# Gathering the running sums into the product's buffer instead of accumulating in the transfer, with 2 MB expert-weight loads

## The reference, cut to what matters

```python
N_EXPERTS, TOP_K, D_FF = 32, 4, 1024      # of 1024 features
# each token's 4 best experts, with softmax gates; for expert e and its tokens:
#   gu  = rows @ w_gate_up[e] + b_gate_up[e]          (1024 -> 2048)
#   a   = clamped swiglu of the even and odd columns  (-> 1024)
#   moe[token] += gate * (a @ w_down[e] + b_down[e])  (1024 -> 1024)
h = layernorm(ALPHA * h + moe)
```

## Time and profile before

| | |
|---|---|
| median of 3 runs | 2167.34 us (2166.53 to 2167.43) |
| profiled execution | 2166.51 us |
| its span, first to last instruction | 2164.7 us |
| TensorE busy | 2074.1 us (96%) |
| VectorE, ScalarE, GpSimd busy | 1304.2, 942.7, 478.6 us |
| mean granted TensorE clock | 0.988 |
| moved by DMA | 540.45 MB, mean 250 GB/s |

### The profile page before, as it was taken

The page is one execution under the profiler, slowest core; times in us unless marked ns, Lnnn a source line. Parts: engine busy times, 40 slices in busy tenths (PEclk is TensorE's granted clock), DMA queues, the critical chain, the costliest instruction groups (busy, mean ns, idle before and its releaser), DMA issues.

```text
span 2164.7 us, 28230 instructions
## 1 busy us (share of the span) xinstructions
PE 2074.1 (96%) x10156; PEld 1542.5 (71%) x10156; DVE 1304.2 (60%) x1467; ACT 942.7 (44%) x1117; POOL 478.6 (22%) x453
## 2 busy tenths in 40 slices
PE   8999999989999998999999999989999999999998
PEld 5778876655566655566655788777777879888887
DVE  7567687664446654456554899873786456423435
ACT  5236354544334553335453677643445423322420
POOL 4261158651212111213322222100220010000000
PEclk9999999999999999999999999999999999999999
DMA  5140177999999999999999999942312333232321
GB/s 202 45 154 21 62 260 309 397 401 414 399 408 408 403 408 408 408 403 411 405 416 407 399 393 382 341 164 79 100 45 79 117 110 124 78 117 78 117 78 39
DMA packets 107513, 540.45 MB, mean 250 GB/s; under 512 B 13012, under 2 KB 14164, under 8 KB 56608
## 3 DMA queue, kind: packets, MB, share of 16 engines
q1 hardware_dynamic: 95184, 507.96, 58.8%
q0 software_dynamic: 9760, 26.47, 4.9%
q10 hardware_dynamic: 2480, 4.80, 0.7%
HBM read 519.26 MB, written 22.28 MB: 250 GB/s over the span
## 4 chain that ended last, share of the span: by engine, by line
PE 75%; DMA 13%; DVE 7%; ACT 2%; issue 1%; POOL 0%; ACTq 0%; DVEq 0%; SPq 0%; POOLq 0%
PE PS L465 71%; DMA ring<-w_down 13%; DVE low L2531 2%; ACT act_parts L1887 1%; PE PS L805 1%; PE PS L880 1%; PE PS L674 0%; DVE st L2283 0%; DVE act_parts L2627 0%; DVE act L2646 0%; DVE act L2642 0%; PE PS L1269 0%; DVE small L2465 0%; PE PS L809 0%; PE PS L473 0%
## 5 line engine op out<-in xcount | busy, mean ns | idle before, releaser
L465 PE MATMUL PS<-act_parts 128*128 128x512 f32 (+2 forms) x2208 | 680.7, 406 | 54.6 <-DVE low L2531 44.1
L2531 DVE TENSOR_TENSOR low<-ring,act_parts 128x2048 fp32r<-128x2048 f32 x224 | 504.8, 2298 | 206.6 <-ACT act_parts L1887 205.9
L1887 ACT ACTIVATE act_parts<-ring 128x2048 fp32r<-128x2048 f32 x228 | 430.3, 1916 | 241.2 <-DMA ring<-w_down 176.8
L465 PEld LDWEIGHTS PS<-act_parts 128*128 128x128 f32 (+2 forms) x2208 | 395.8, 192 | 154.7 <-DVE low L2531 47.4
L465 PE MATMUL PS<-act_parts,ring_parts 128*128 128x512 f32 (+3 forms) x1696 | 466.8, 374 | 0.0
L465 PE MATMUL PS<-low,act_parts 128*128 128x512 f32 x960 | 382.7, 399 | 0.0
L465 PEld LDWEIGHTS PS<-act_parts,ring_parts 128*128 128x128 f32 (+1 forms) x1696 | 302.2, 187 | 67.0 <-issue 13.3
L465 PE MATMUL PS<-ring,act 128*64 128x512 f32 (+1 forms) x1274 | 288.9, 595 | 0.0
L465 PE MATMUL PS<-ring_parts,act_parts 128*128 128x512 f32 (+2 forms) x1208 | 271.0, 381 | 2.1 <-DVE act_parts L3030 2.1
L465 PEld LDWEIGHTS PS<-ring_parts,act_parts 128*128 128x128 f32 (+1 forms) x1208 | 218.3, 187 | 48.6 <-issue 4.7
L465 PE MATMUL PS<-ring_parts 128*128 128x512 f32 (+1 forms) x672 | 250.7, 380 | 0.0
(11 more groups left out here) (340 smaller groups left out, 1887.2 us busy)
## 6 DMA issues: line engine op xcount, KB each, us to landing
ring<-w_gate_up SPq DMA_DIRECT2D x264, 1024.0 KB, 21.0
ring<-w_down SPq DMA_DIRECT2D x132, 1024.0 KB, 21.5
ring<-w_ff SPq DMA_DIRECT2D x16, 2048.0 KB, 7.8
ring<-w_in SPq DMA_DIRECT2D x12, 2048.0 KB, 10.4
ring<-w_o SPq DMA_DIRECT2D x1, 4096.0 KB, 14.5
ring<-w_out SPq DMA_DIRECT2D x2, 2048.0 KB, 7.7
acc_d<-ring POOLq DMA_DIRECT2D x5, 512.0 KB, 5.8
act<-x SPq DMA_DIRECT2D x4, 512.0 KB, 5.7
```

Of the source, the lines that this page charges most:

```text
L465: return eng.matmul(o, lhsT, rhs, start=first, stop=last, **kw)
L1887: A_(W1hi[c % CS], W1[c], ACT.Copy).then_inc(sem["high"], 1)
L2531: tt(W1lo[c], W1[c], W1hi[c % CS].bitcast(F32), ALU.subtract).then_inc(sem["low"], 1)
```

## The change

GpSimd now also gathers the rows of the sums that an item's product will be added to. `name_product(i-1)` stands in step i in place of `name_gate`: it names the gate, waits until the write of item i-2 has landed (`added`), copies the row numbers of item i-1 to `to_c`, and issues an indirect gather of those rows of `acc_d` into `yb` (`sums_in`). `take_product` moves from ScalarE to VectorE and multiplies the product by its gate and adds it to what stands in `yb`; in a big step it comes after `chunk_low` of chunk 5, in a small step after `act_low`. `add_product` writes `yb` back by a plain indirect transfer. Row numbers out of bounds are skipped in both, and the spare region of `acc_d` goes. GpSimd's order in a step becomes `add_product`, `over_table`, `name_product`, `next_rows`, `next_select`. The expert weights are laid out so that two chunks are one load of 2 MB, 16 KB a partition, with one semaphore a pair, issued when both places are free. The last steps follow the same pattern.

```diff
@@ SyncE
+            def load_pair(e, n):
+                eng.dma_start(ring[:, 2 * n * BW:2 * (n + 1) * BW], pair_src(e, n)).then_inc(sem[f"pair_in{n}"], 16)
...
             def gate_up_loads(i, e):
-                for c in range(8):
-                    eng.wait_ge(sem["gate_up_used"], 8 * i + (c - 7))
-                    load_chunk(e, c)
+                for n in range(4):
+                    eng.wait_ge(sem["gate_up_used"], 8 * i + (2 * n - 6))
+                    load_pair(e, n)
...
@@ ScalarE
             def big_item(i, at):
...
-                if at > 1:
-                    take_product(i, at)
...
@@ VectorE
+            def take_product(i, at):
+
+                eng.wait_ge(sem["down_used"], 4 * i)
+                eng.wait_ge(sem["gate_named"], i - 1)
+                eng.wait_ge(sem["sums_in"], 16 * i - 16)
+                if is_small(at - 2):
+                    stt(yb[:, 0:512], PS[:, 4, :], gate_c, yb[:, 0:512], ALU.mult, ALU.add).then_inc(
+                        sem["down_free"], 1)
+                else:
+                    stt(yb, PS[:, 4:6, :].rearrange("p a b -> p (a b)"), gate_c, yb, ALU.mult, ALU.add).then_inc(
+                        sem["down_free"], 1)
...
                 for c in range(4, 8):
                     chunk_low(i, at, c)
+                    if c == 5 and at > 1:
+                        take_product(i, at)
...
@@ GpSimd
+            def name_product(i, at):
+
                 e = column(i, at)
+                gates, places = (small_list[:, E:], to_small) if is_small(at) else (slot_gate, to_i)
                 eng.sem_inc(sem["pool_passed"], 1)
                 eng.tensor_copy(gate_c, gates[:, bass.ds(e, 1)]).then_inc(sem["gate_named"], 1)
+                eng.wait_ge(sem["added"], 16 * i + 16)
+                eng.sem_inc(sem["pool_passed"], 1)
+                eng.tensor_copy(to_c[:, :], places[:, bass.ds(e, 1)]).then_inc(sem["places_named"], 1)
+                eng.wait_ge(sem["places_named"], i + 1)
+                eng.sem_inc(sem["pool_passed"], 1)
+                sums, x, last = (acc_halves, yb[:, 0:512], 2 * S - 1) if is_small(at) else (acc_d, yb, S - 1)
+                eng.indirect_dma_start(out=x, out_offset=None, in_=sums,
+                                       in_offset=bass.IndirectOffsetOnAxis(ap=to_c[:, 0:1], axis=0),
+                                       bounds_check=last, oob_is_err=False).then_inc(sem["sums_in"], 16)
...
             def add_product(i, at):
-                e = column(i - 2, at - 2)
                 eng.wait_ge(sem["down_free"], i)
                 eng.sem_inc(sem["pool_passed"], 1)
...
                 eng.indirect_dma_start(out=sums, out_offset=bass.IndirectOffsetOnAxis(ap=to_c[:, 0:1], axis=0),
-                                       in_=x, in_offset=None, compute_op=ALU.add).then_inc(sem["added"], 16)
+                                       in_=x, in_offset=None, bounds_check=last, oob_is_err=False).then_inc(
+                                           sem["added"], 16)
...
             def step(i, at):
+                add_product(i, at)
+                if 1 < at < NT + 2:
+                    over_table(at - 2)
+                name_product(i - 1, at - 1)
                 e = column(i + 1, at + 1)
                 next_rows(i, at, e)
-                if 1 < at < NT + 2:
-                    over_table(at - 2)
-                add_product(i, at)
-                name_gate(i - 1, at - 1)
                 next_select(i, at, e)
```

More of the change, by code:

```diff
@@ L163, in build @@
         h1_d, x2_d = dram("h1_d", (S, D)), dram("x2_d", (S, D))
[L164 removed]
+        acc_d = dram("acc_d", (S, D))
         acc_halves = acc_d.rearrange("r (h c) -> (r h) c", h=2)
@@ L418, in place_last, with chunk_in @@
             return {"gate_up": c if c < 4 else c - 2, "before": (c - 4) % CS, "down": c - 8}[kind]
+        def chunk_in(i, at, c, ahead=0):
+            if at == 0 and c < 4:
+                return sem[f"expert_in{c}"], 16
+            return sem[f"pair_in{c // 2}"], 16 * i + (0 if c < 4 else 16 if c < 8 else ahead)
         where = {}
@@ L1503, in chunk_place, with pair_src @@
                 return W1[c].rearrange("p (k c) -> p k c", k=2)
+            def pair_src(e, n):
+                if n < 4:
+                    return A["w_gate_up"][bass.ds(e, 1)][:, n].rearrange("o p x -> (o p) x")
+                return A["w_down"][0][bass.ds(e, 1)].rearrange("o (h m j) d -> h (o m) (j d)", h=2, m=P)[n - 4]
+            def load_pair(e, n):
+                eng.dma_start(ring[:, 2 * n * BW:2 * (n + 1) * BW], pair_src(e, n)).then_inc(sem[f"pair_in{n}"], 16)
             eng.dma_start(HN[0:META, 4, :], A["meta_tokens"]).then_inc(signal("x4_in", 16), 16)
@@ L1557, in _ @@
                 eng.dma_start(bd[m * E:(m + 1) * E, :], A["b_down"][0]).then_inc(signal("router_in", 16), 16)
-            def load_chunk(e, c):
-                eng.dma_start(chunk_place(c), chunk_src(e, c)).then_inc(sem[f"expert_in{c}"], 16)
             def gate_up_loads(i, e):
-                for c in range(8):
-                    eng.wait_ge(sem["gate_up_used"], 8 * i + (c - 7))
-                    load_chunk(e, c)
+                for n in range(4):
+                    eng.wait_ge(sem["gate_up_used"], 8 * i + (2 * n - 6))
+                    load_pair(e, n)
             def down_loads(i, e):
-                for c in range(8, CH):
-                    eng.wait_ge(sem["down_used"], 4 * i + (c - 11))
-                    load_chunk(e, c)
+                for n in range(4, CS):
+                    eng.wait_ge(sem["down_used"], 4 * i + (2 * n - 10))
+                    load_pair(e, n)
             eng.wait_ge(*past("ln1_out", 1))
@@ L1580, in _ @@
             eng.wait_ge(*past("mix_psum", 16))
[L1581 to L1588, removed]
+            for n in range(2, 5):
+                load_pair(0, n)
+            gate_up_loads(1, 1)
+            eng.wait_ge(*past("sums_begun", 64))
+            load_pair(0, 5)
             eng.wait_ge(*past("items_ordered", 3))
@@ L1961, in act_high @@
                     A_(aThi[:, hh, :], PS[:, 6 + hh, :], ACT.Copy).then_inc(sem[f"aT_high{hh}"], 1)
[L1963 to L1974, removed]
             def big_item(i, at):
@@ L2049, in last_high @@
             def last_high(kind, c):
-                landed = {"gate_up": 16, "before": 0, "down": 16}[kind]
-                eng.wait_ge(sem[f"expert_in{c}"], 16 * final + landed)
+                eng.wait_ge(*chunk_in(final, LAST, c, {"gate_up": 0, "before": 0, "down": 16}[kind]))
                 place = place_last(kind, c)
@@ L2816, in _ @@
                 act_low(final, LAST, hh)
+            take_product(final, LAST)
             for c in range(8, CH):
@@ L2822, in _ @@
             act_low(final + 1, LAST, 0)
+            take_product(final + 1, LAST + 1)
             for c in range(8, 11):
@@ L3346, in add_product @@
             def add_product(i, at):
-                e = column(i - 2, at - 2)
                 eng.wait_ge(sem["down_free"], i)
                 eng.sem_inc(sem["pool_passed"], 1)
[L3350 to L3354, removed]
+                sums, x, last = (acc_halves, yb[:, 0:512], 2 * S - 1) if is_small(at - 2) else (acc_d, yb, S - 1)
                 eng.indirect_dma_start(out=sums, out_offset=bass.IndirectOffsetOnAxis(ap=to_c[:, 0:1], axis=0),
-                                       in_=x, in_offset=None, compute_op=ALU.add).then_inc(sem["added"], 16)
+                                       in_=x, in_offset=None, bounds_check=last, oob_is_err=False).then_inc(
+                                           sem["added"], 16)
             def next_select(i, at, e):
@@ L3395, in _ @@
             list_small()
-            name_gate(0, 0)
-            eng.wait_ge(*past("sums_begun", 80))
+            eng.wait_ge(*past("sums_begun", 64))
+            name_product(0, 0)
             for i in range(2, NT + 3):
@@ L3412, in _ @@
             add_product(final, LAST)
-            name_gate(final - 1, LAST - 1)
+            name_product(final - 1, LAST - 1)
             eng.wait_ge(sem["rows_in"], 16 * final)
@@ L3539 @@
     w = arrays["w_gate_up"].reshape(E, P, 4, 2, 2, P, 2, 2, 2)
-    arrays["w_gate_up"] = np.ascontiguousarray(w.transpose(0, 4, 2, 1, 3, 6, 5, 7, 8)).reshape(E, 8, P, BW)
+    w = w.reshape(E, P, 2, 2, 2, 2, P, 2, 2, 2)
+    arrays["w_gate_up"] = np.ascontiguousarray(w.transpose(0, 5, 2, 1, 3, 4, 7, 6, 8, 9)).reshape(E, 4, P, 2 * BW)
     b = arrays["b_gate_up"].reshape(1, E, 2, P, 2, 4)
```

15 lines of the change are left out of this document (5 added, 10 removed).

## The result

The changed kernel takes 2534.09 us (median of 4 runs, 2532.41 to 2537.37), the kernel before 2167.39 us beside it: 1.1691 times as long (95% interval 1.1677 to 1.1705), 367 us more. The forecast was 2405 us with a range of 2290 to 2500: slower, as said, but by 367 us where some 239 were forecast, and outside the range.

A forecast was written before the change was run, and what follows sets the result against it. The weight stream was taken to bound the small and big steps, TensorE close behind. 2166.5 + 187 (13 pairs) + 47 (four end steps) + 5 (the rest) = 2405 us, range 2290 to 2500.

The forecast's parts named there:

- the loop: Each step chains product, take, write, sums, rows, turn, `down`; TensorE waits for late rows: +14.4 us a pair.
- a slow clock after each wait: TensorE's turn and `down` after waiting for rows run partly at half speed, losing 1.6 us each time.
- three quarters of the way: Pair cost set between lightest and loaded landings, as weights stream three quarters of the time: 0.8 + 0.75 x 18.1 = +14.4 us.
- the lightest load: All four landings of a pair at 5.1 us, the shortest found in the trace: +0.8 us a pair.
- the loaded prices: Landings as loaded as before: small write 8.9, rows of 128 8.5 plus 1.7, big write 11.5, rows of 64 7.9 us.
- the rival of longer landings: Weight packets twice as long stretch a pair's four landings by 10.4 us: +22.2 a pair, 2525 us; chance 0.14.
- The 13 pairs: Small and big steps of items 2 to 27, at +14.4 us a pair: +187 us.
- The four steps at the end: Big items, steps 28 to 31, wait for rows too: +11.7 us each, +47 us.
- 5 for the rest: Later last write before the layer norm and waiting for two free places: +5 us together.
- rival "hidden": Rows land before TensorE asks, the lighter weight stream sets the pace: -18 to -57 us, 2130 us; chance 0.06.

The follow-up runs named there:

- rows first: The changed kernel with `next_rows` moved back to the head of GpSimd's step, ahead of `add_product`; 2160.44 us, 0.9965 of the kernel before.
- weights held: The changed kernel with an item's gate and up loads held back until its token rows have landed (item 1 excepted); 2364.76 us, 1.0906 of the kernel before.
- all four kernels that gained: Rows first with 2 MB (2160.44 us) or 1 MB loads (2160.95); the kernel before with 2 MB loads alone (2161.29) or also skipping empty slots (2159.82).
- late rows alone: The kernel before with the rows' gather moved behind the adding transfer and the gate's name, no landing wait or sums' gather; 2176.43 us, 1.0037.

## Why the prediction was off

**Right: the loop.** Rows asked for after the landing, TensorE waiting for them before L811 and L815, a DMA share near 0.8 (measured 0.77) and a slow clock after each wait were forecast, and rows first shows that this is the whole cause: without the loop nothing is lost. Counted on fixed parts the forecast holds within a microsecond. From the small product to its write it had 3.0 us (measured 924.46 - 920.88 = 3.6), from the big product (read, as in the earlier trace rows, at the start of the last L886, 965.18) to its write 10.5 (975.80 - 965.18 = 10.6). What is left of a pair without its four landings was forecast at 79.7 - 34.0 = 45.7 us and measured at 88.9 - 42.5 = 46.4.

**Wrong: the size of the landings, "three quarters of the way".** The forecast put the four landings of a pair between 20.4 us at the lightest load and 38.5 as loaded in the earlier trace rows, and took three quarters of the way by the mean share of the stream: 34.0. The share itself was right; the step that failed is to price the landings by it, and to hold the loads of 2 MB to be harmless to them. They took 42.5, 8.5 more, and that is most of the 9.2 us by which a pair was missed (88.9 against 79.7). Step by step, against the loaded prices: small write 8.0 (8.9), rows of 128 behind the sums 14.9 (10.2), big write 10.4 (11.5), rows of 64 9.2 (7.9). Two things are in the 8.5.

- *The 2 MB loads, 6.3 us a pair and 94 us in all.* The forecast counted them as relief ("The loads of 2 MB and the cheaper transfers relieve the stream") and gave their effect on the landings no price; 1 MB loads in the changed kernel show that they lengthen them. This is the rival of longer landings, held at 0.14 and priced at 10.4 us a pair. It was the nearest case (2525), but in part by luck: it had 7.8 us for the packets, where 6.3 were measured, and 34.0 for the load, where 36.25 were measured, and the two errors nearly cancel. The Trainium skill (DMA: Bandwidth & Descriptors, section "Queues, rings and completion order") says that an engine goes round its queues a packet at a time; shorter landings at half the load size agree with it, if the packets that it means are those that the profile counts, which no run here shows. Whether the size of a packet or the two chunks that come at once do it is not told apart by these runs.
- *The mean share, 2.2 us a pair.* With 1 MB loads, the same as in the kernel before, the landings still took 36.25, not 34.0. The idle quarter of the stream falls into `down`, where no landing is. The windows above show it, and weights held turns it round: the same loads moved to another place in the step take 14.5 us off the landings. That this explains all of the 2.2 us is argued and not shown. Thirteen times 2.2 is 29 of the other 35 of the 129 us; the rest was not traced further.

In the rows' landing of a small step the queue's order comes in too: 14.90 us behind the sums' gather, 10.69 ahead of it, where the forecast allowed 1.7 for the sums. With 1 MB loads it took 10.01 behind the sums, close to the 10.2 forecast: the price of this place in the queue held for the smaller loads. What the rows take ahead of the sums with 1 MB loads was not run.

**Where the 367 us lie.** The adds of the kernel before and the writes of the changed one can be matched by their order. These are the first, the 27th and the 31st of 32 (items 0, 26 and 30), before and after:

```profile
376.93 1.66 POOL L3355 DMA_INDIRECT acc_d<-act,to_c  x1 [0.84 <-POOL to_c L3351]
1229.28 3.50 POOL L3355 DMA_INDIRECT acc_d<-act,to_c  x1 [0.80 <-POOL to_c L3351]
1369.33 1.58 POOL L3355 DMA_INDIRECT acc_d<-act,to_c  x1 [0.83 <-POOL to_c L3351]
...
384.73 1.05 POOL L3367 DMA_INDIRECT acc_d<-act,to_c  x1 [11.90 <-DVE act L2651]
1550.55 2.23 POOL L3367 DMA_INDIRECT acc_d<-act,to_c  x1 [29.13 <-DVE act L2648]
1740.96 2.21 POOL L3367 DMA_INDIRECT acc_d<-act,to_c  x1 [25.94 <-DVE act L2651]
```

The 13 pairs take 1165.8 us instead of 852.4, 313 more (forecast 187). The four steps at the end take 190.4 instead of 140.1, 50 more (forecast 47). Ahead of the first write 8 us are lost, and behind the 31st 4 are gained (forecast 5 for the rest). So the forecast missed in the pairs, and there alone.

**The clock.** In 910.36 to 924.00 and in 950.80 to 965.00, each behind a wait of 11.03 and 14.67 us, the granted clock was 0.84 and 0.83 while TensorE worked without a gap: part of each stretch at 1.2 instead of 2.4 GHz. L815 takes 1.97 us, where its like took 1.16 in the earlier trace rows. By these two numbers that loses 13.64 x 0.16 = 2.2 and 14.20 x 0.17 = 2.4 us, where the forecast had 1.6 each time.

**The rival "hidden" was also mispriced.** Rows first is that case: the rows land before TensorE asks. It gave 2160 where the rival said 2130. GpSimd's queue took 6.4% of 700 us instead of 8.2, 12.6 us less where 15 were forecast, but the weights moved in 700 us rose only from 271.10 to 271.74 MB at a share of 1.00. So the stream didn't hand the freed time on. Its chain of waits still stands 29.2% on loads of `w_down` (32.6% in the kernel before), with TensorE busy for 662.6 of 700 us. What holds a pair of rows first at 64.4 us (875.29 to 1004.06 for two), and all four kernels that gained within 0.1% of one another, stays open. That larger packets save up to 4.9%, as the rival allowed, is not borne out, since 2 MB loads alone gave 0.26%.

## What to carry to other kernels

Before moving a call on an engine that issues transfers, write down the ring that it closes: here late rows alone cost 8 us with an early take, a landing to be waited for cost nothing, and the two in one ring cost 264 us on top (2439.96 - 2176.43, sums' gather and VectorE's take with them), before the 2 MB loads added 94. Price a transfer in such a ring by the load in the stretch where it runs, not by the mean over the loop, because the waits themselves push the loads into that stretch. And ask of larger loads what they do to the small transfers beside them: the edit that gained at most 6 us with the landings covered lost 94 us with them in the ring.

## What the runs showed of the hardware beyond what was expected

- The landing of one and the same gather of 64 rows took 9.21 us beside the weight stream and 3.27 with the weights held, under the 5.1 that I had taken as the lightest. The Trainium skill (DMA: Bandwidth & Descriptors, section "Anatomy of one DMA — SWDGE (gpsimd) path") gives some 2.0 us and the bytes at 436 GB/s, 2.6 as an estimate for all 64 rows of 4 KB. With the weights held the trace comes near it (3.27); beside the stream it disagrees (9.21).
- Holding loads back made a kernel 169 us faster, with 16.21 us of load put on its chain in each pair.
- Skipping empty slots in the adding transfer cut the share of GpSimd's queue in 700 us from 8.3% to 6.4% with nearly the same packets (5609 and 5554), and the hardware queue's share rose by 1.1 points for the same 272.7 MB. The kernel got no faster.
